# Attention weights normalized on VectorE and transposed in transpose mode, with the products of two heads alternating on halves of the array

## The chip, the cores and the metric

One core of a Trainium2 chip. The metric is device time in microseconds of one execution. TensorE is called PE below, VectorE DVE, ScalarE ACT, GpSimd POOL and SyncE SP, as in the profile. PE's clock is granted at one of two levels, 2.4 GHz (the profile writes 1.00) and 1.2 GHz (0.50).

## The reference

A two-layer decoder trunk over 1040 positions (16 meta tokens and 1024 inputs) of width 1024: a state-space mixer with a gated output, a mixture of experts, sliding-window attention, a second mixture of experts, and a final norm. The change touches the attention:

```python
scale = HEAD_DIM ** -0.5                        # 16 heads of 64, 4 heads of keys and values
s_band = einsum('bnqkgd,bnskd->bnkgqs', qb, k_band) * scale   # own block of 128 and the one before it
s_meta = einsum('bnqkgd,bmkd->bnkgqm', qb, k_meta) * scale    # 16 meta tokens, always visible
s_band = where(band_ok, s_band, NEG)            # 0 <= query position - key position < 128
probs = softmax(concatenate([sink, s_meta, s_band], axis=-1), axis=-1)
o = einsum(p_meta, v_meta) + einsum(p_band, v_band)
return o @ w_o + b_o
```

The sink is one learned logit for each head; it takes part in the sum of the softmax and has no value.

## The kernel before, in words

The program runs its phases one after another with a barrier between them: `phase_ssm`, `phase_glu`, `phase_moe` for layer 0, `phase_project` (keys, values, queries), `phase_attend`, and `phase_moe` for layer 1 with the final norm. Each phase writes out one program for each engine; the order in it is the order in which the engine works, and semaphores join the engines.

`phase_attend` takes 64 steps (`NS`). A step `s` is one query tile of 128 positions (`i = s // 8`) and one pair of heads (`c = s % 8`). Queries and keys stand transposed: the first head of the pair in partitions 0 to 63, the second in 64 to 127. In tile 0 a step has two blocks of keys (the 16 meta tokens and its own block of 128), from tile 1 on three (with the block before). A step goes through:

- PE, `scores(s)`: for each head, a product for every block of keys, with a contraction over 64 rows. The two heads use the two halves of the array's rows.
- DVE, `scores(s)`: adds the mask while reading the scores of both heads (L1888), then takes the negated maximum (L1892), the sink included, which POOL has copied beside the scores (L1831).
- ACT, `exps(s)`: exponentials and their sums, one instruction for each head (L1846).
- DVE, `divisors(s)`: the reciprocals of the sums (L1896), and a diagonal matrix for each head, the identity times the reciprocal (L1900).
- PE, `transpose_weights(s)`: ordinary float32 products of the weights with this diagonal matrix, which transpose and normalize at once (L1963, L1965, L1966).
- ACT, `copy_weights(s)`: copies the transposed weights out of PSUM (L1855, L1856).
- PE, `outputs(s)`: values times transposed weights, three products for each head in one accumulation (L1977, L1979, L1980). Each head has 64 output partitions, that is a half of the array's columns.
- ACT and DVE: `o_hi_part` (L1863) and `o_lo_part` (L1907) split the outputs into two parts for the projection.

`project(i, half)` on PE multiplies a finished tile with half of the output weights, 24 products of 512 columns (L1992 to L1994). DVE adds the result to the residual stream (`add_projection`, L1914). In the first eight steps ACT and DVE also split the output weights that SP loads (L1873, L1928).

The orders are written out by hand. PE: `scores(s + 1)`, `outputs(s - 1)`, `transpose_weights(s)`, and behind the steps `c = 3` and `c = 6` a projection of the tile before. DVE: `o_lo_part(s - 2)`, `divisors(s)`, `scores(s + 1)`, and an addition of a projection at `c = 4` and `c = 7`. ACT: `o_hi_part(s - 2)`, `exps(s)`, `copy_weights(s - 1)`. Scores, weights and their transposed copies are double-buffered; the PSUM tile of the transposes (`ps_t`) and that of the outputs (`ps_o`) are single. POOL adds the output bias to the residual stream once for each tile (L1835).

Of the kernel before, what the change touches and what calls it, by code (L numbers as in the profile page):

```python
# [12 lines left out]
ALU = mybir.AluOpType  # L13
# [1739 lines left out]
def phase_attend(nc, t):  # L1753
# [10 lines left out]
    with ExitStack() as ctx:  # L1764
# [3 lines left out]
        def ps(name, shape):  # L1768
# [5 lines left out]
        mask = sb("mask", [P, SC_W])  # L1774
        sinks = sb("sinks", [P, N_HEADS])
# [8 lines left out]
        diag = sb("diag", [P, 2, H2, P])  # L1784
# [11 lines left out]
        sc_mm, sm_done, nm_done, exp_done, rinv_done, diag_done, pt_mm, pt_done, pv_mm, o_hi_done, o_lo_done, y_mm, h_done = (  # L1796
            sem(x) for x in ("sc_mm", "sm_done", "nm_done", "exp_done", "rinv_done", "diag_done", "pt_mm",
                             "pt_done", "pv_mm", "o_hi_done", "o_lo_done", "y_mm", "h_done"))

        def width(s):  # L1800

            return SC_W if s >= DC else N_META + P
# [13 lines left out]
        def _(pool):  # L1816
# [4 lines left out]
            pool.wait_ge(mask_step, 1)  # L1821
            G_.affine_select(out=mask[:, N_META:N_META + P], in_=mask[:, N_META:N_META + P], compare_op=ALU.is_ge,
                             fill=NEG, base=0, pattern=[[-1, P]], channel_multiplier=1).then_inc(mask_step, 1)
            G_.affine_select(out=mask[:, N_META + P:], in_=mask[:, N_META + P:], compare_op=ALU.is_gt,
# [54 lines left out]
        def _(dve):  # L1879
            V = nc.vector  # L1880

            def scores(s):

                dve.wait_ge(sc_mm, s + 1)
                if s >= 2:
                    dve.wait_ge(exp_done, 2 * (s - 1))
                w = width(s)
                V.tensor_tensor(sm[:, s % 2, :, 1:1 + w], ps_s[:, 2 * (s % 2):2 * (s % 2) + 2, 0:w],  # L1888
                                mask[:, 0:w].unsqueeze(1).to_broadcast([P, H2, w]), ALU.add).then_inc(sm_done, 1)
# [27 lines left out]
            dve.wait_ge(mask_step, 3)  # L1917
            scores(0)
            for s in range(NS):
# [3 lines left out]
                divisors(s)  # L1923
# [14 lines left out]
        def _(pe):  # L1938
            T = nc.tensor

            def scores(s):
# [3 lines left out]
                for r in range(2):  # L1945
                    rows = slice(r * DH, (r + 1) * DH)
                    out = ps_s[:, 2 * (s % 2) + r, :]
                    q = q_t[rows, c, i * P:(i + 1) * P]
                    k = k_t[rows, c // 2, :]
                    T.matmul(out[:, 0:N_META], q, k[:, XT * P:TOK], start=True, stop=True)  # L1950
                    last = T.matmul(out[:, N_META:N_META + P], q, k[:, i * P:(i + 1) * P], start=True, stop=True)
                    if i:
                        last = T.matmul(out[:, N_META + P:SC_W], q, k[:, (i - 1) * P:i * P], start=True, stop=True)  # L1953
                last.then_inc(sc_mm, 1)

            def transpose_weights(s):
                i = s // DC
                pe.wait_ge(diag_done, s + 1)
                if s:
                    pe.wait_ge(pt_done, s)  # L1960
                for r in range(2):
                    p, d = pr[:, s % 2, r, :], diag[:, s % 2, r, :]
                    T.matmul(ps_t[:, r, 0:P], p[:, 1 + N_META:1 + N_META + P], d, start=True, stop=True)  # L1963
                    if i:
                        T.matmul(ps_t[:, r, P:2 * P], p[:, 1 + N_META + P:1 + SC_W], d, start=True, stop=True)  # L1965
                    last = T.matmul(ps_t[0:N_META, r, 2 * P:3 * P], p[:, 1:1 + N_META], d, start=True, stop=True)  # L1966
                last.then_inc(pt_mm, 1)

            def outputs(s):
# [5 lines left out]
                for r in range(2):  # L1975
# [68 lines left out]
```

## Time and profile before

| | |
|---|---|
| median of 3 runs | 2682.65 us (2681.4 to 2683.64) |
| span of the profiled execution | 2682.4 us |
| its own time | given by its span alone; 0.2 us under the median |
| PE busy over the span | 2226.1 us (83%) |
| DVE busy | 1691.0 us (63%) |
| ACT busy | 1242.7 us (46%) |
| POOL busy | 569.7 us (21%) |
| attention phase | from 1488 to 1927 us |

Busy time is what the instructions of an engine cover. Products on PE are pipelined and their recorded lengths overlap, so the time from one start to the next says what one costs. A float32 product is recorded as two passes, each with its own load of the stationary tile (PEld); a product of the rounded float32 form and a transpose in transpose mode are recorded as one.

### The profile page before, as it was taken

What the parts mean: (1) busy time and instruction counts of PE and PEld (TensorE: products, weight loads), DVE (VectorE), ACT (ScalarE), POOL (GpSimd) and SP (SyncE); (2) the same over time, 40 slices, a digit from 0 to 9 for tenths busy, and PEclk for the clock granted to TensorE, in tenths of its full rate; (3) what the DMA queues carried; (4) which work ended last, traced back from release to release, by engine and by line L of the source; (5) the groups of instructions that cost most, each with busy time, mean ns of one, the idle gap of its engine ahead of it and who ended that gap; (6) DMA issues with size and microseconds to landing.
All of it is one profiled execution on the core that took longest, in us unless ns stands there. A gap on an engine that the chain in (4) does not pass through costs nothing. (4 is left out here: it accounts for less than half of the span.)

```text
span 2682.4 us, 32669 instructions
## 1 busy us (share of the span) xinstructions
PE 2226.1 (83%) x11052; PEld 1744.2 (65%) x11052; DVE 1691.0 (63%) x1593; ACT 1242.7 (46%) x1431; POOL 569.7 (21%) x735
## 2 busy tenths in 40 slices
PE   2380489983999999997399999999857999999992
PEld 2130467772788888886288567777655888888881
DVE  6987042126788888885622434444255888888885
ACT  3020341031677777775200323333224777777772
POOL 2105000012233333331210100000021212333333
PEclk9965799966999999998599579999958999999996
DMA  5819550041899999995410200000144999999985
GB/s 157 84 32 84 118 179 32 1 168 56 305 365 376 369 367 372 376 373 222 149 48 24 71 1 1 1 1 1 54 161 142 354 361 372 381 379 377 385 322 234
DMA packets 156509, 527.02 MB, mean 196 GB/s; under 512 B 37072, under 2 KB 87440, under 8 KB 105088
## 3 DMA queue, kind: packets, MB, share of 16 engines
q1 hardware_dynamic: 138000, 492.13, 53.4%
q0 software_dynamic: 18432, 33.86, 3.4%
q8 instruction: 49, 0.80, 0.1%
q14 instruction: 28, 0.23, 0.0%
HBM read 497.42 MB, written 55.71 MB: 206 GB/s over the span
## 5 line engine op out<-in xcount | busy, mean ns | idle before, releaser
L1347 DVE TENSOR_TENSOR moe_lo<-moe_raw,moe_hi 128x2048 fp32r<-128x2048 f32 x378 | 861.6, 2293 | 127.0 <-ACT moe_hi L1152 118.8
L1152 ACT CAST moe_hi<-moe_raw 128x2048 fp32r<-128x2048 f32 x374 | 714.3, 1914 | 154.8 <-PE moe_ps_g L1476 76.1
L1474 PE MATMUL moe_ps_y<-moe_hi,moe_h_hi 128*128 128x512 f32 x512 | 210.0, 410 | 11.0 <-DVE moe_h_lo L1363 11.0
L1474 PE MATMUL moe_ps_g<-moe_hi,moe_x_hi 128*128 128x512 f32 x512 | 212.3, 415 | 7.4 <-DVE moe_x_lo L1352 4.7
L1475 PE MATMUL moe_ps_g<-moe_hi,moe_x_lo 128*128 128x512 f32 x512 | 206.3, 403 | 0.0
L1476 PE MATMUL moe_ps_g<-moe_lo,moe_x_hi 128*128 128x512 f32 x512 | 206.1, 402 | 0.0
L1475 PE MATMUL moe_ps_y<-moe_hi,moe_h_lo 128*128 128x512 f32 x512 | 204.5, 400 | 0.0
L1476 PE MATMUL moe_ps_y<-moe_lo,moe_h_hi 128*128 128x512 f32 x512 | 204.3, 399 | 0.0
L1476 PE MATMUL moe_ps_u<-moe_lo,moe_x_hi 128*128 128x512 f32 x512 | 203.0, 396 | 0.0
L1475 PE MATMUL moe_ps_u<-moe_hi,moe_x_lo 128*128 128x512 f32 x512 | 202.8, 396 | 0.0
L1474 PE MATMUL moe_ps_u<-moe_hi,moe_x_hi 128*128 128x512 f32 x512 | 202.8, 396 | 0.0
L1159 ACT CAST moe_x_hi<-moe_ps_xt 128x1024 fp32r<-128x1024 f32 x64 | 65.0, 1016 | 212.7 <-PE moe_ps_xt L1461 212.7
L785 PE MATMUL glu_acc<-glu_w_hi,glu_z_hi 128*128 128x512 f32 (+1 forms) x288 | 115.6, 401 | 36.2 <-DVE glu_w_lo L750 30.9
L1888 DVE TENSOR_TENSOR att_sm<-att_ps_s,att_mask 128x544 f32<-128x544 f32 (+1 forms) x64 | 44.2, 691 | 146.1 <-PE att_ps_s L1953 133.6
L1096 POOL TENSOR_TENSOR moe_unit<-moe_mhalf 128x1 f32<-128x1 f32 x64 | 20.4, 318 | 508.5 <-DMA y_dram<-moe_y,moe_si 508.5
L1863 ACT CAST att_o_hi<-att_ps_o 128x128 fp32r<-128x128 f32 x64 | 17.0, 265 | 226.3 <-PE att_ps_o L1980 226.3
L1076 POOL COPY moe_gi<-moe_idx_in 128x1 int32 x64 | 80.2, 1254 | 186.3 <-issue 109.3
L1352 DVE TENSOR_TENSOR moe_x_lo<-moe_ps_xt,moe_x_hi 128x1024 fp32r<-128x1024 f32 x64 | 78.4, 1224 | 64.7 <-ACT moe_x_hi L1159 64.7
L1474 PEld LDWEIGHTS moe_ps_g<-moe_hi,moe_x_hi 128*128 128x128 f32 x512 | 99.5, 194 | 30.0 <-DVE moe_x_lo L1352 5.5
L1474 PEld LDWEIGHTS moe_ps_y<-moe_hi,moe_h_hi 128*128 128x128 f32 x512 | 97.8, 191 | 32.6 <-DVE moe_lo L1347 11.4
L1079 POOL TENSOR_TENSOR moe_unit<-moe_mhalf 128x1 f32<-128x1 f32 x128 | 113.6, 888 | 10.8 <-POOL moe_gi L1076 0.2
L787 PE MATMUL glu_acc<-glu_w_lo,glu_z_hi 128*128 128x512 f32 (+1 forms) x288 | 114.4, 397 | 0.0
(347 smaller groups left out, 4660.8 us busy)
## 6 DMA issues: line engine op xcount, KB each, us to landing
moe_raw<-moe_w_gate SPq DMA_DIRECT2D x128, 1024.0 KB, 6.7
moe_raw<-moe_w_up SPq DMA_DIRECT2D x128, 1024.0 KB, 9.2
moe_raw<-moe_w_down SPq DMA_DIRECT2D x128, 1024.0 KB, 8.2
moe_raw<-y_dram SPq DMA_DIRECT2D x16, 1024.0 KB, 11.6
glu_w_raw<-ssm_w_glu SPq DMA_DIRECT2D x8, 1024.0 KB, 5.9
xn_dram<-moe_work SPq DMA_DIRECT2D x16, 512.0 KB, 6.1
u_dram<-ssm_reg SPq DMA_DIRECT2D x8, 520.0 KB, 5.0
ssm_reg<-u_dram SPq DMA_DIRECT2D x8, 520.0 KB, 21.4
```

The lines of the kernel that those rows point to most:

```text
L785: nc.tensor.matmul(out, zh, wh, start=(c == 0), stop=False)
L787: return nc.tensor.matmul(out, zh, wl, start=False, stop=(c == DC - 1))
L1076: G_.tensor_copy(dst[:, :], idx[:, bass.ds(c, 1)]).then_inc(ix_step, 1)
L1079: G_.tensor_tensor(unit[:, 0:1], mhalf[:, :], mhalf[:, :], ALU.mult)
L1152: A.copy(hi[:, slot(number, k), :], raw[:, k, :]).then_inc(hi_done, 1)
L1159: A.copy(x_hi[:, :, :].rearrange("p c m -> p (c m)"), ps_xt[:, :]).then_inc(xt_hi, 1)
L1347: V.tensor_tensor(lo[:, slot, :], raw[:, k, :], hi[:, slot, :].bitcast(F32), ALU.subtract).then_inc(lo_done, 1)
L1352: V.tensor_tensor(x_lo[:, :, :].rearrange("p c m -> p (c m)"), ps_xt[:, :], x_hi[:, :, :].bitcast(F32).rearrange("p c m -> p (c m)"), ALU. ...
L1474: T.matmul(out, x_h, w_h, start=first, stop=False)
L1475: T.matmul(out, x_l, w_h, start=False, stop=False)
L1476: return T.matmul(out, x_h, w_l, start=False, stop=final)
L1888: V.tensor_tensor(sm[:, s % 2, :, 1:1 + w], ps_s[:, 2 * (s % 2):2 * (s % 2) + 2, 0:w], mask[:, 0:w].unsqueeze(1).to_broadcast([P, H2, w]), ...
```

## The change

DVE no longer builds diagonal matrices. `normalize(s)` multiplies the weights of each head in place with the reciprocal of their sum (two instructions over 144 columns in tile 0, 272 from tile 1 on), and PE transposes them in transpose mode against the identity. The order of the columns in the scores changes, so that the block before comes ahead of the own block: both are one product of 256 columns. For tile 0, which has no block before, there is a second mask, `mask0`. In `scores` and `outputs` the two heads' products alternate: the same block for the first head, then for the second. The orders between the steps stay.

```diff
-        diag = sb("diag", [P, 2, H2, P])
+        mask0 = sb("mask0", [P, N_META + P])
...
+            G_.memset(mask0[:], 0.0).then_inc(mask_step, 1)
+            pool.wait_ge(mask_step, 2)
+            for own in (mask0[:, N_META:], mask[:, N_META + P:]):
+                G_.affine_select(out=own, in_=own, compare_op=ALU.is_ge, fill=NEG, base=0, pattern=[[-1, P]],
+                                 channel_multiplier=1).then_inc(mask_step, 1)
+            G_.affine_select(out=mask[:, N_META:N_META + P], in_=mask[:, N_META:N_META + P], compare_op=ALU.is_gt,
                              fill=NEG, base=0, pattern=[[1, P]], channel_multiplier=-1).then_inc(mask_step, 1)
...
-            def divisors(s):
+            def normalize(s):
                 dve.wait_ge(exp_done, 2 * (s + 1))
                 V.reciprocal(rinv[:, s % 2, :], rs[:, s % 2, :]).then_inc(rinv_done, 1)
                 dve.wait_ge(rinv_done, s + 1)
-                if s >= 2:
-                    dve.wait_ge(pt_mm, s - 1)
-                V.tensor_tensor(diag[:, s % 2], ident[:, :].unsqueeze(1).to_broadcast([P, H2, P]),
-                                rinv[:, s % 2, :].unsqueeze(2).to_broadcast([P, H2, P]),
-                                ALU.mult).then_inc(diag_done, 1)
+                for r in range(H2):
+                    p = pr[:, s % 2, r, 1:1 + width(s)]
+                    V.tensor_scalar(p, p, rinv[:, s % 2, r:r + 1], None, ALU.mult).then_inc(norm_done, 1)
...
             def scores(s):
...
-                for r in range(2):
-                    T.matmul(out[:, 0:N_META], q, k[:, XT * P:TOK], start=True, stop=True)
-                    last = T.matmul(out[:, N_META:N_META + P], q, k[:, i * P:(i + 1) * P], start=True, stop=True)
-                    if i:
-                        last = T.matmul(out[:, N_META + P:SC_W], q, k[:, (i - 1) * P:i * P], start=True, stop=True)
+                lo, w = (max(i - 1, 0) * P, min(i + 1, 2) * P)
+                for out, rows in zip(outs, halves):
+                    T.matmul(out[:, N_META:N_META + w], q_t[rows, c, i * P:(i + 1) * P], k_t[rows, c // 2, lo:lo + w],
+                             start=True, stop=True)
+                for out, rows in zip(outs, halves):
+                    last = T.matmul(out[:, 0:N_META], q_t[rows, c, i * P:(i + 1) * P], k_t[rows, c // 2, XT * P:TOK],
+                                    start=True, stop=True)
...
             def transpose_weights(s):
-                    T.matmul(ps_t[:, r, 0:P], p[:, 1 + N_META:1 + N_META + P], d, start=True, stop=True)
+                    T.transpose(ps_t[:, r, 0:P], p[:, own:own + P], ident[:])
                     if i:
-                        T.matmul(ps_t[:, r, P:2 * P], p[:, 1 + N_META + P:1 + SC_W], d, start=True, stop=True)
-                    last = T.matmul(ps_t[0:N_META, r, 2 * P:3 * P], p[:, 1:1 + N_META], d, start=True, stop=True)
+                        T.transpose(ps_t[:, r, P:2 * P], p[:, 1 + N_META:1 + N_META + P], ident[:])
+                    last = T.transpose(ps_t[0:N_META, r, 2 * P:3 * P], p[:, 1:1 + N_META], ident[:])
...
             def outputs(s):
-                for r in range(2):
-                    out, w = ps_o[r * DH:(r + 1) * DH, 0:P], pt[:, s % 2, r, :]
-                    T.matmul(out, v_sb[:, i, vc], w[:, 0:P], start=True, stop=False)
-                    if i:
-                        T.matmul(out, v_sb[:, i - 1, vc], w[:, P:2 * P], start=False, stop=False)
-                    last = T.matmul(out, v_sb[0:N_META, XT, vc], w[0:N_META, 2 * P:], start=False, stop=True)
+                for r in range(H2):
+                    T.matmul(outs[r], v_sb[:, i, vc], w[r][:, 0:P], start=True, stop=False)
+                if i:
+                    for r in range(H2):
+                        T.matmul(outs[r], v_sb[:, i - 1, vc], w[r][:, P:2 * P], start=False, stop=False)
+                for r in range(H2):
+                    last = T.matmul(outs[r], v_sb[0:N_META, XT, vc], w[r][0:N_META, 2 * P:], start=False, stop=True)
```

## Rows read from the trace of the kernel before

**Rows 1.** Stages of attention: window, length, busy time (count) by engine, clock, DMA.
```profile
1499.70:1530.50 30.80, 30.80 (x122) 16.73 (x121) 14.64 (x30) 13.19 (x41) 0.93 (x5) 0.50 0.28 86
1545.60:1563.10 17.50, 17.50 (x74) 11.83 (x72) 4.69 (x11) 4.24 (x14) 0.38 (x3) 0.50 0.00 1
1602.20:1653.10 50.90, 50.90 (x337) 36.42 (x336) 22.00 (x43) 16.95 (x56) 3.83 (x9) 1.00 0.00 1
```
**Rows 2.** Waits from 1480 to 1915: total us, times, longest.
```profile
DVE att_sm L1888 <- PE att_ps_s L1953: 133.6, 56, 8.4
...
PE att_ps_t L1963 <- DVE att_diag L1900: 3.2, 1, 3.2
```
**Rows 3.** Timeline of PE over one step: start, us, then operation.
```profile
1737.34 0.39 PE L1950 MATMUL att_ps_s<-k_t,q_t 64*128 64x16 f32 x2
...
1738.45 0.43 PE L1977 MATMUL att_ps_o<-att_pt,v_sb 128*64 128x128 f32 x2
...
1740.33 0.49 PE L1963 MATMUL att_ps_t<-att_diag,att_pr 128*128 128x128 f32 x2
...
1742.25 0.28 PE L1950 MATMUL att_ps_s<-k_t,q_t 64*128 64x16 f32 x1
```
**Rows 4.** Timeline: transposes in the MoE stage, and column halves in the state stage.
```profile
2020.54 0.27 PE L1453 MATMUL moe_ps_ht<-moe_ident,moe_over 128*1 128x128 f32 x1 [1.32 <-DVE moe_over L1330]
...
2020.65 0.27 PE L1454 MATMUL moe_ps_ht<-moe_ident,moe_over 128*1 128x128 f32 x1
...
133.16 0.67 PE L623 MATMUL ssm_psr<-ssm_reg,ssm_vt 128*64 128x130 f32 x8
133.76 0.33 PE L613 MATMUL ssm_pst<-ssm_ident,ssm_reg 128*128 128x128 f32 x1
```
**Rows 5.** Timeline of DVE and ACT over the same step.
```profile
1738.56 0.72 DVE L1888 TENSOR_TENSOR att_sm<-att_ps_s,att_mask 128x544 f32<-128x544 f32 x1 [1.10 <-PE att_ps_s L1953]
1739.32 0.72 DVE L1892 TENSOR_REDUCE att_nm<-att_sm 128x2 f32<-128x546 f32 x1
...
1740.43 0.27 ACT L1863 CAST att_o_hi<-att_ps_o 128x128 fp32r<-128x128 f32 x1 [2.15 <-PE att_ps_o L1980]
1740.59 0.53 ACT L1846 ACTIVATE att_pr<-att_sm,att_nm 128x273 f32<-128x273 f32 x1
...
1741.75 0.17 DVE L1896 RECIPROCAL att_rinv<-att_rs 128x2 f32<-128x2 f32 x1 [0.73 <-ACT att_pr L1846]
1741.95 0.43 DVE L1900 TENSOR_TENSOR att_diag<-att_ident,att_rinv 128x256 f32<-128x256 f32 x1
...
1742.36 0.59 ACT L1855 COPY att_pt<-att_ps_t 128x512 f32<-128x512 f32 x1 [0.64 <-PE att_ps_t L1966]
1742.84 0.36 ACT L1856 COPY att_pt<-att_ps_t 16x256 f32<-16x256 f32 x1
```
**Rows 6.** Groups by line: scalings on DVE, busy us, mean ns.
```profile
L467 DVE TENSOR_SCALAR ssm_pw_n<-ssm_pw_i 128x288 f32<-128x288 f32 x1 | 0.3, 309 | 0.0
```
**Rows 7.** Timeline of PE over a step at the lower clock.
```profile
1556.29 0.61 PE L1950 MATMUL att_ps_s<-k_t,q_t 64*128 64x16 f32 x2
...
1558.32 0.69 PE L1977 MATMUL att_ps_o<-att_pt,v_sb 128*64 128x128 f32 x2
...
1561.64 0.80 PE L1963 MATMUL att_ps_t<-att_diag,att_pr 128*128 128x128 f32 x2
```
**Rows 8.** Clock and busy time in other stages, columns as in rows 1.
```profile
120.00:154.00 34.00, 28.16 (x284) 17.39 (x280) 27.58 (x52) 11.92 (x30) 0.97 (x1) 1.00 0.17 36
1935.80:1939.20 3.40, 3.40 (x18) 3.40 (x17) 0.84 (x1) 1.63 (x2) 0.00 (x0) 0.50 0.91 255
1939.20:1942.60 3.40, 2.46 (x23) 2.35 (x22) 1.41 (x3) 2.38 (x5) 1.58 (x5) 1.00 0.94 320
1942.60:1963.00 20.40, 20.40 (x100) 20.40 (x99) 6.79 (x9) 8.24 (x12) 7.55 (x27) 0.50 0.96 391
...
2055.20:2058.60 3.40, 3.40 (x9) 2.64 (x8) 2.30 (x2) 0.53 (x1) 0.00 (x0) 0.50 1.03 434
```

More of the change, by code:

```diff
@@ L1795, in phase_attend @@
                              "w_lo_done"))
-        sc_mm, sm_done, nm_done, exp_done, rinv_done, diag_done, pt_mm, pt_done, pv_mm, o_hi_done, o_lo_done, y_mm, h_done = (
-            sem(x) for x in ("sc_mm", "sm_done", "nm_done", "exp_done", "rinv_done", "diag_done", "pt_mm",
+        sc_mm, sm_done, nm_done, exp_done, rinv_done, norm_done, pt_mm, pt_done, pv_mm, o_hi_done, o_lo_done, y_mm, h_done = (
+            sem(x) for x in ("sc_mm", "sm_done", "nm_done", "exp_done", "rinv_done", "norm_done", "pt_mm",
                              "pt_done", "pv_mm", "o_hi_done", "o_lo_done", "y_mm", "h_done"))
@@ L1887, in scores @@
                 w = width(s)
+                visible = mask if s >= DC else mask0
                 V.tensor_tensor(sm[:, s % 2, :, 1:1 + w], ps_s[:, 2 * (s % 2):2 * (s % 2) + 2, 0:w],
-                                mask[:, 0:w].unsqueeze(1).to_broadcast([P, H2, w]), ALU.add).then_inc(sm_done, 1)
+                                visible[:, :].unsqueeze(1).to_broadcast([P, H2, w]), ALU.add).then_inc(sm_done, 1)
                 dve.wait_ge(sm_done, s + 1)
@@ L1916, in _ @@
             dve.wait_ge(ident_step, 2)
-            dve.wait_ge(mask_step, 3)
+            dve.wait_ge(mask_step, 5)
             scores(0)
@@ L1922, in _ @@
                     o_lo_part(s - 2)
-                divisors(s)
+                normalize(s)
                 if s + 1 < NS:
@@ L1944, in scores @@
                     pe.wait_ge(sm_done, s - 1)
-                for r in range(2):
[L1946 to L1949, printed above, removed]
-                    T.matmul(out[:, 0:N_META], q, k[:, XT * P:TOK], start=True, stop=True)
-                    last = T.matmul(out[:, N_META:N_META + P], q, k[:, i * P:(i + 1) * P], start=True, stop=True)
-                    if i:
-                        last = T.matmul(out[:, N_META + P:SC_W], q, k[:, (i - 1) * P:i * P], start=True, stop=True)
+                outs = [ps_s[:, 2 * (s % 2) + r, :] for r in range(H2)]
+                halves = [slice(r * DH, (r + 1) * DH) for r in range(H2)]
+                lo, w = (max(i - 1, 0) * P, min(i + 1, 2) * P)
[5 more added lines that the diff above has]
+                                    start=True, stop=True)
                 last.then_inc(sc_mm, 1)
@@ L1974, in outputs @@
                 vc = slice((c // 2) * DH, (c // 2 + 1) * DH)
-                for r in range(2):
-                    out, w = ps_o[r * DH:(r + 1) * DH, 0:P], pt[:, s % 2, r, :]
-                    T.matmul(out, v_sb[:, i, vc], w[:, 0:P], start=True, stop=False)
-                    if i:
-                        T.matmul(out, v_sb[:, i - 1, vc], w[:, P:2 * P], start=False, stop=False)
-                    last = T.matmul(out, v_sb[0:N_META, XT, vc], w[0:N_META, 2 * P:], start=False, stop=True)
+                outs = [ps_o[r * DH:(r + 1) * DH, 0:P] for r in range(H2)]
+                w = [pt[:, s % 2, r, :] for r in range(H2)]
+                for r in range(H2):
[3 more added lines that the diff above has]
+                        T.matmul(outs[r], v_sb[:, i - 1, vc], w[r][:, P:2 * P], start=False, stop=False)
+                for r in range(H2):
+                    last = T.matmul(outs[r], v_sb[0:N_META, XT, vc], w[r][0:N_META, 2 * P:], start=False, stop=True)
                 last.then_inc(pv_mm, 1)
```

9 lines of the change are left out of this document (3 added, 6 removed).

## The prediction

> **What bounds the kernel now.** I began with the busy rows of the stages of the attention phase [rows 1]. The reader is to see that PE is busy in every microsecond of each of them, while DVE and ACT are busy less than half. The row of a whole query tile lasts 50.9 us with the granted clock at 1.00, that is 2.4 GHz. The first tile (30.8 us for five steps, 6.16 each) and the second tile's first steps (17.5 us for two, 8.75 each) have it at 0.50, 1.2 GHz. Next the waits: the add of the scores on DVE waits for PE, 134 us in all, and PE waits for DVE once, 3.2 us [rows 2]. So PE's own order sets the time of the phase, and nothing outside the phase is touched: a microsecond won there is won at the end.
>
> The timeline of PE over one step, a pair of heads, [rows 3] gives 4.91 us and its parts: scores 1.11 (1737.34 to 1738.45), outputs 1.88 (to 1740.33), transposes 1.92 (to 1742.25). Eight such steps make 39.3 of a tile's 50.9 us, so each of its two projections costs 5.8. Every product appears as two passes (x2), and a 128-column pass takes 0.11 us.
>
> **The change on PE.** *Transposes.* Six products of two passes become six of one: the transposes of the MoE stage start 0.11 us apart with one record each, although their stationary tile is a single column [rows 4], so 0.11 is the price of streaming 128 columns once. 6 x 0.11 = 0.66 off: 1.92 becomes 1.26. Whether the 16-column one still forces a pause between shapes is not shown; without pauses it would be about 0.9, and if the transpose saved nothing 1.92. I take 1.26, the row's form with one pass gone.
> *Outputs.* Today head 0's three products and head 1's three stand one behind the other, 0.94 each. Six passes make only 0.66 of that; the other 0.28 are an uncovered load and two pauses, about 0.09 each, where the shape changes from 128 rows to 16 and back. In the state stage eight passes of 130 columns for the two column halves go through between 133.16 and 133.76 [rows 4]: 0.60 us, pause included, where eight times 0.11 is 0.88. So halves of equal shape overlap; in attention the 16-row product between the heads keeps them apart. Alternating puts equal shapes side by side: 0.94 + 0.03 = 0.97. The other end, no overlap, saves only two of the four changes of shape with their pauses: 1.6.
> *Scores.* The two row halves overlap already, head 1 starting about a quarter microsecond late. Four products instead of six: a head is one load 0.11, two passes of 256 columns (estimate: 2 x 0.21), two short ones with a load, 0.13, and the pause of 0.09, so 0.75, plus 0.06 lag: 0.81. The bound above is today's 1.11.
> PE's sum: 1.26 + 0.97 + 0.81 = 3.04 us, for 4.91.
>
> **The change on DVE, and the new bound.** PE would drop under the loop that runs from exponentials to exponentials, hidden until now. From [rows 5]: exponentials to reciprocal 1741.75 - 1740.59 = 1.16; reciprocal to the next operation 0.20; then the diagonal product (0.43) is replaced by two scalings of 272 columns. A scaling of 288 columns took 0.309 [rows 6]; I take 0.30 for each, less 0.08 that neighbours without a wait between them overlap (an estimate; on ACT L1856 is recorded 0.11 before the end of L1855): 0.44 for the two. The slow end, each scaling at the diagonal's 0.43, adds 0.28. The add of the next scores could then start 1.80 after the exponentials. Add to reduce 0.76, reduce 0.72 and hand-over 0.04: 3.32.
> ACT's loop: two exponentials of 0.51, then the copies 0.48 + 0.36, hand-over 0.12 (estimate), which is 1.98; outputs to the rounding 1.08 (today 1740.43 less the second head's start, half of 1.88 before 1740.33; and 0.03), rounding to exponentials 0.16: 3.22. PE's order adds a tie: it starts outputs at 1.98, ends them at 2.95 and the transposes at 4.21, 0.83 into the next step, so the scores behind them reach DVE at 0.83 + 0.81 + 0.21 = 1.85 instead of 1.80: 3.37. With loops of 3.04, 3.22 and 3.37 so closely interlocked I take a step of 3.4 us; the bounds are 3.3 and, with slow scalings, 3.65, and without overlap of the halves 3.8.
>
> Scaling 0.44 instead of 0.35 for the diagonal was free before under PE's cover; now it is on the path, some 0.1 us in each step. The wait that goes (the diagonal's on the transposes two steps back) was always met. The normalized weights are written in place, so nothing new is queued behind another buffer. GpSimd's addition of the output bias collides with the seventh step's scaling as it did with the diagonal, and lies under the projection, 5.8 us. The second mask is two more GpSimd operations of 0.3 us before the first step: 0.5 us lost once. Operand order of the masks costs nothing.
>
> A step across a projection: when its exponentials start PE has 0.83 of transposes left, then 5.7 of projection, the next scores arrive 1.02 later, and add and reduce follow, 1.52: 9.07. A tile becomes 6 x 3.4 + 2 x 9.07 = 38.5 us for 50.9: 12.4 less, for six tiles 74 us.
>
> **The stretch at 1.2 GHz.** There a step of the second tile splits into scores 2.03, outputs 3.32, transposes 3.4 [rows 7]. The same cuts: transposes less 6 x 0.21 = 2.1, outputs 1.7, scores 1.5: 5.3, over DVE's loop, so PE sets it. The first tile's 6.16 becomes 4.0 by the same working with two thirds of the products. Gains: five steps of 2.1 in the first tile, 10 (the first two are start-up); two mixed ones after it, 4.7; three of the second tile at 3.1 (the first is partly narrow), 9.3; the step with the first projection 1.5 only, because the projection may have to bring the clock up: in the MoE stage it stood at 0.50 through a row of dense products (the row at 2055.2) [rows 8]. The rest of the tile has the full clock, four steps of 1.5: 6. Together 31 us.
>
> **Sum.** 74 + 31 - 0.5 = 104.5, and about 1 for the tail, of a span of 2682.4; the median of the runs shown, 2682.65, is 0.2 us above it. I forecast 2580 us rather than 2577, the tight interlocking costing a few hundredths of a microsecond in each step.
>
> **Rivals.**
> 1. *Halves don't overlap, or slow scalings.* For: the two streams read all 128 rows at once with full weights here. Against: [rows 4]. With a step of 3.8 a tile is 6 x 3.8 + 2 x 9.47 = 41.7, six tiles give 55 and the slow stretch, where the outputs keep 2.9 of their 3.3, some 19: 2608. Slow scalings alone, a step of 3.65, give 2592; both together about 2625.
> 2. *The clock falls between projections.* PE would for the first time have gaps, about a tenth of each step. For: in the row at 1939.2 the clock was 1.00 with PE busy 2.46 of 3.4 us, and in the next it is 0.50 again. Against: from 120 to 154 us it stayed at 1.00 with PE busy 28.2 of 34 us, in a loop of transposes and half-width products like the new step; and it rose right behind 3.4 us in which nearly all of PE's 18 records were transposes (the row at 1935.8) [rows 8]. If it falls, a step costs 5.3, 1.9 more, and a projection that has to bring the clock back costs 3 more (up to 6 us at half speed, an estimate from the row at 2055.2). With n such steps a tile is 38.5 + 1.9 n + 6. The 31 us won in the slow stretch allow a tile of 56, so it decides from six steps of the eight: 2683 there, 2706 with all eight. This is the case on the other side.
> The Trainium skill, "TensorE: Matmul & The Clock Gate", Part 4, says that transposes do not count as activity for the clock, which speaks against this change. By that rule rival 2 would happen. The trace does not agree: the clock rose behind the row at 1935.8, where PE was busy 3.40 of 3.40 us with transposes.
> 3. *An earlier rise.* Denser passes bring 1.00 already in the second tile's first steps: 10 us less, 2570.
> 4. *The change doesn't do what it says*: transposes go through in two passes. PE then needs 3.7 and holds the copy up: a step of 3.95, 2614.
>
> **Chances.** Forecast, 2566 to 2597: 0.62. Rival 3, 2555 to 2566: 0.07. Rival 1, 2592 to 2625: 0.16. Rival 4: 0.04. Rival 2 in part, up to 2677: 0.06; from six steps on 0.05, of which 0.01 within the measurement's reach of 2683. The range leaves out rival 2 above 2628 and what lies below rival 3: 2555 to 2628, 0.85. What a measurement of this kernel can tell from no change is 0.2%, 5.4 us. Faster 0.94, same 0.02, slower 0.04, the last two from rival 2.
>
> **What the profile after would show.** A tile of 38.5 us with clock 1.00; transposes as single records 0.11 apart; heads' outputs starting within 0.05 of each other; PE for the first time waiting, about 0.35 us a step, mostly before the outputs or the transposes; DVE busy 2.4 of 3.4 us; scalings of 0.30. Wrong would be: the two heads' outputs 0.5 or more apart in their ends, scalings of 0.44, PEclk under 1.00 between 1600 and 1850 us, or a wait I don't see, such as DVE held by GpSimd's copies in every step.

## The result and the profile after

The changed kernel takes 2554.08 us (median of 4 runs, 2552.01 to 2557.14) against 2683.14 (4 runs, 2681.40 to 2686.24) beside it: a ratio of 0.952, 95% interval 0.9506 to 0.9533. It is 129 us faster, where 103 were forecast, and it lies 1 us under the forecast's range of 2555 to 2628. Its profiled execution has a span of 2552.1 us and a time of 2553.88, so the profile speaks for the runs.

First the same stages as in [rows 1], now of the changed kernel: most of tile 0, the two rows of the profile on either side of the clock's rise, and one whole tile from its first reduce to that of the next. The columns are the length, then the busy time of each engine with its number of instructions, the granted clock, and the DMA share.

```profile
core 0: us, PE busy (x) PEld busy (x) DVE busy (x) ACT busy (x) POOL busy (x), PEclk, DMA share, GB/s
1500.00:1522.10 22.10, 21.78 (x131) 13.60 (x132) 20.38 (x46) 16.85 (x50) 3.42 (x7) 0.50 0.45 143
1525.80:1529.20 3.40, 3.40 (x22) 2.69 (x22) 1.92 (x6) 2.15 (x7) 0.19 (x1) 0.50 0.00 0
1529.20:1532.60 3.40, 2.69 (x32) 1.97 (x28) 2.44 (x7) 2.11 (x7) 0.19 (x1) 1.00 0.00 0
1559.65:1596.61 36.96, 31.77 (x260) 23.80 (x256) 22.36 (x51) 16.92 (x56) 3.85 (x9) 1.00 0.00 1
```

A tile lasts 36.96 us instead of 50.90, and PE, busy without a gap before, now idles for 5.2 us of it. The clock rises at 1529.2 us, in the third step of tile 1; before, it stood at 0.50 until 1574.0, when the first projection ran.

The waits of the attention phase, in answer to [rows 2]: total, times, longest.

```profile
ACT att_o_hi L1865 <- PE att_ps_o L1985: 133.3, 63, 5.8
DVE att_sm L1891 <- PE att_ps_s L1953: 49.7, 17, 4.7
DVE att_rinv L1899 <- ACT att_pr L1848: 47.6, 56, 1.0
PE att_ps_o L1980 <- ACT att_pt L1858: 37.5, 43, 1.6
```

DVE waited 133.6 us for scores; now it does so 17 times, nearly all behind the projections, and in the steps between it waits for the exponentials. PE waits in 43 steps for the copied weights. In a step of tiles 1 to 7 that crosses no projection, each of PE, DVE and ACT now waits for another: no engine is the bound, a chain through two of them is.

PE over one step right behind a projection, where its parts stand close together as in [rows 3] (start, length):

```profile
1668.87 0.70 PE L1950 MATMUL att_ps_s<-k_t,q_t 64*128 64x256 f32 x4
1669.41 0.29 PE L1953 MATMUL att_ps_s<-k_t,q_t 64*128 64x16 f32 x4
1669.63 0.44 PE L1980 MATMUL att_ps_o<-att_pt,v_sb 128*64 128x128 f32 x4
1669.90 0.39 PE L1983 MATMUL att_ps_o<-att_pt,v_sb 128*64 128x128 f32 x4
1670.22 0.43 PE L1985 MATMUL att_ps_o<-att_pt,v_sb 16*64 16x128 f32 x4
1670.59 0.33 PE L1965 MATMUL att_ps_t<-att_ident,att_pr 128*128 128x128 f32 x1
1670.75 0.27 PE L1967 MATMUL att_ps_t<-att_ident,att_pr 128*128 128x128 f32 x1
1670.86 0.27 PE L1968 MATMUL att_ps_t<-att_ident,att_pr 128*16 128x128 f32 x1
1670.97 0.27 PE L1965 MATMUL att_ps_t<-att_ident,att_pr 128*128 128x128 f32 x1
...
1671.39 0.49 PE L1950 MATMUL att_ps_s<-k_t,q_t 64*128 64x256 f32 x2
```

Scores 0.76, outputs 0.96, transposes 0.80: 2.52 us for 4.91. The transposes are single records, and the 16-column one (L1968) is followed after 0.11 like every other.

The loop through DVE and ACT, from exponentials to exponentials, in answer to [rows 5]; first DVE, then ACT:

```profile
1672.42 0.17 DVE L1899 RECIPROCAL att_rinv<-att_rs 128x2 f32<-128x2 f32 x1 [0.39 <-ACT att_pr L1848]
1672.62 0.63 DVE L1903 TENSOR_SCALAR att_pr<-att_pr,att_rinv 128x272 f32<-128x272 f32 x2
1673.17 0.72 DVE L1891 TENSOR_TENSOR att_sm<-att_ps_s,att_mask 128x544 f32<-128x544 f32 x1
1673.92 0.72 DVE L1895 TENSOR_REDUCE att_nm<-att_sm 128x2 f32<-128x546 f32 x1
```

```profile
1671.27 0.53 ACT L1848 ACTIVATE att_pr<-att_sm,att_nm 128x273 f32<-128x273 f32 x1 [0.30 <-DVE att_nm L1895]
1672.29 0.56 ACT L1857 COPY att_pt<-att_ps_t 128x512 f32<-128x512 f32 x1
1674.68 0.52 ACT L1848 ACTIVATE att_pr<-att_sm,att_nm 128x273 f32<-128x273 f32 x1 [0.18 <-DVE att_nm L1895]
```

It takes 1.15 us from the exponentials to the reciprocal, 0.20 to the scalings, 0.55 to the add, 0.75 to the reduce and 0.76 to the next exponentials: 3.41 in all, which is the plain step. A step across a projection takes 8.24 (a crossing, below), and six of the one and two of the other make the tile.

**Where the 130.3 us between the two spans come from**, by the starts of the reduces (a tile is eight intervals between them):

| stretch | before | after | change | forecast |
|---|---|---|---|---|
| up to the first reduce | 1491.0 | 1494.0 | +3.0 | +0.5 |
| tile 0 | 44.6 | 28.1 | -16.4 | -10 |
| tile 1 | 66.6 | 37.6 | -29.1 | -21 |
| tiles 2 to 7, to the end of the phase | 325.1 | 240.3 | -84.9 | -75 |
| second mixture of experts | 755.1 | 752.1 | -3.0 | 0 |

The last row is the same code in both, and so is nearly all of the first: in the twelve kernels below the attention phase starts between 1486.6 and 1494.3 us, and the last phase takes 751.6 to 754.8 (755.1 before is just above). I take both rows for scatter. The 0.5 us that the forecast charged for the second mask did not appear: from the first scores to the first reduce it is 2.84 us before and 2.85 after, because the reduce waits for the copied sinks in both. The forecast's two steps of mixed width, 4.7 us, stand in its row of tile 1; by the reduces one of them (7.27 us before, 5.33 after) lies in tile 0.

### The profile page after: what moved, and what is told of

The parts are those of the page before. It is cut to its first block and busy times, and to the rows that moved or that the text cites. A ratio compares the mean times of both kernels' runs of the same rounds, so it can differ in the third digit from the quotient of the medians.

```text
span 2552.1 us, 31490 instructions
## 1 busy us (share of the span) xinstructions
PE 2056.5 (81%) x10460; PEld 1636.8 (64%) x10460; DVE 1693.2 (66%) x1657; ACT 1242.0 (49%) x1431; POOL 564.4 (22%) x737
## 5 line engine op out<-in xcount | busy, mean ns | idle before, releaser
L1096 POOL TENSOR_TENSOR moe_unit<-moe_mhalf 128x1 f32<-128x1 f32 x64 | 16.4, 256 | 514.1 <-DMA y_dram<-moe_y,moe_si 514.1
L1476 PEld LDWEIGHTS moe_ps_g<-moe_lo,moe_x_hi 128*128 128x128 f32 x512 | 98.9, 193 | 24.2
L786 PE MATMUL glu_acc<-glu_w_hi,glu_z_lo 128*128 128x512 f32 (+1 forms) x288 | 114.1, 396 | 0.0
L1079 POOL TENSOR_TENSOR moe_unit<-moe_mhalf 128x1 f32<-128x1 f32 x128 | 111.5, 871 | 10.7
```

The lines of the kernel that those rows point to most:

```text
L786: nc.tensor.matmul(out, zl, wh, start=False, stop=False)
L1079: G_.tensor_tensor(unit[:, 0:1], mhalf[:, :], mhalf[:, :], ALU.mult)
L1476: return T.matmul(out, x_h, w_l, start=False, stop=final)
```

## The experiments

All are edits of the changed kernel; every step that TensorE, VectorE or ScalarE takes for the output stays. The table has the medians, the ratio to before with its interval, the plain step and the step across a projection of tiles 2 to 7, and when the clock rose in the attention phase.

| kernel | us | ratio | step | across | clock 1.00 at |
|---|---|---|---|---|---|
| changed kernel | 2554.1 | 0.9520 (0.9506 to 0.9533) | 3.41 | 8.24 | 1529.2 |
| a_diag_alternate | 2600.5 | 0.9690 (0.9674 to 0.9706) | 3.88 | 9.67 | 1540.4 |
| b_transposes_alone | 2616.6 | 0.9757 (0.9740 to 0.9773) | 4.05 | 9.51 | 1555.6 |
| c_outputs_serial | 2606.1 | 0.9716 (0.9699 to 0.9732) | 4.05 | 9.16 | 1551.8 |
| e_scores_serial | 2560.9 | 0.9543 (0.9527 to 0.9559) | 3.41 | 8.58 | 1544.2 |
| d_one_scaling | 2554.1 | 0.9523 (0.9510 to 0.9536) | 3.50 | 8.15 | 1529.4 |
| f_scores_first | 2543.2 | 0.9484 (0.9469 to 0.9498) | 3.13 | 8.12 | 1527.4 |
| h_three_orders | 2526.4 | 0.9407 (0.9393 to 0.9422) | 2.52 | 8.32 | 1542.8 |
| g_transposes_x4 | 2555.3 | 0.9525 (0.9511 to 0.9540) | 3.41 | 8.24 | 1503.0, lost 1530.3 to 1533.8 |
| i_fill_whole | 2523.9 | 0.9404 (0.9389 to 0.9418) | 2.52 | 8.32 | 1501.6 |
| j_fill_half | 2557.7 | 0.9531 (0.9517 to 0.9546) | 2.52 | 8.32 | 1578.7 |
| k_after_again | 2556.2 | 0.9528 (0.9515 to 0.9541) | 3.41 | 8.24 | 1527.4 |
| l_fill_less | 2525.1 | 0.9403 (0.9384 to 0.9423) | 2.52 | 8.32 | 1495.0, lost 1522.3 to 1546.2 |

### One part undone at a time

**a_diag_alternate**: the diagonal back in place of the scalings.

```diff
-                for r in range(H2):
-                    p = pr[:, s % 2, r, 1:1 + width(s)]
-                    V.tensor_scalar(p, p, rinv[:, s % 2, r:r + 1], None, ALU.mult).then_inc(norm_done, 1)
+                V.tensor_tensor(diag[:, s % 2], ident[:, :].unsqueeze(1).to_broadcast([P, H2, P]),
+                                rinv[:, s % 2, :].unsqueeze(2).to_broadcast([P, H2, P]), ALU.mult).then_inc(norm_done, 1)
...
-                    T.transpose(ps_t[:, r, 0:P], p[:, own:own + P], ident[:])
+                    T.matmul(ps_t[:, r, 0:P], p[:, own:own + P], d, start=True, stop=True)
```

> The changed kernel with its alternating outputs and merged scores, but with the diagonal product on VectorE and ordinary transposing products on TensorE, as before. If the parts measured on TensorE simply add (scores 0.76, outputs 0.96, transposes back at 1.92), TensorE needs 3.64 us a step and is never idle: a tile of 8 x 3.64 + 2 x 5.8 = 40.7 us instead of 36.96, some 25 us over tiles 1 to 7, so about 2580 us if the clock still rises during tile 0, and about 2605 if the early rise came from the transpose mode and is lost with it. Rival: the loop through VectorE alone sets the step and the transposes were free already; then the step stays at 3.3 to 3.4 and the time at or under 2555.

Measured: 2600.5 us, 46 more than the changed kernel. The step behind a projection is 3.64, the sum of the parts to the hundredth, but the others take 3.88. The trace shows why:

```profile
1579.83 0.49 PE L1968 MATMUL att_ps_t<-att_diag,att_pr 128*128 128x128 f32 x2
...
1581.87 0.59 ACT L1858 COPY att_pt<-att_ps_t 128x512 f32<-128x512 f32 x1 [0.47 <-PE att_ps_t L1971]
...
1582.76 0.44 PE L1983 MATMUL att_ps_o<-att_pt,v_sb 128*64 128x128 f32 x4 [0.17 <-ACT att_pt L1859]
...
1583.71 0.49 PE L1968 MATMUL att_ps_t<-att_diag,att_pr 128*128 128x128 f32 x2
```

Transposes 2.04 with the hand-over, copies 0.89, outputs 0.95: a loop of 3.88 through PE and ACT, longer than PE's sum, because the scores (0.76) that PE does meanwhile are shorter than the hand-over and the copies. The expectation that the parts simply add was short by it; the rival, in which the transposes were free, falls. The clock rose 11 us later than in the changed kernel, but at the same place in the work: while PE worked on the third set of wide scores of tile 1 or on the outputs right behind it, ahead of the projection. So the early rise does not need the transpose mode.

**b_transposes_alone**: scores and outputs back in the order of before (`+ for r in range(H2):` around all three products of a head, in both). **c_outputs_serial**: the outputs alone:

```diff
                 for r in range(H2):
                     T.matmul(outs[r], v_sb[:, i, vc], w[r][:, 0:P], start=True, stop=False)
-                if i:
-                    for r in range(H2):
+                    if i:
                         T.matmul(outs[r], v_sb[:, i - 1, vc], w[r][:, P:2 * P], start=False, stop=False)
-                for r in range(H2):
                     last = T.matmul(outs[r], v_sb[0:N_META, XT, vc], w[r][0:N_META, 2 * P:], start=False, stop=True)
```

> Only the scalings and the transposes of the change; scores and outputs in the order of before. TensorE's parts would be 0.80 + 1.88 + 1.11 = 3.79 a step; the loop through ScalarE (exponentials 1.02, copies 0.84, outputs 1.88, rounding to exponentials 0.2, hand-overs 0.1) would be about 4.05. If the loop holds, a step of 4.05 and a tile of about 42.5 us: 2590 us with an early rise of the clock, about 2630 if the rise needs the alternating halves (then it comes as late as before, near 1574 us). If only TensorE's sum matters, a step of 3.8 and some 10 us less.

> The changed kernel with only the outputs back in serial order, one head behind the other. TensorE's sum is 0.76 + 1.88 + 0.80 = 3.44, no more than today's step of 3.41: if TensorE's sum or VectorE's loop is what counts, the time stays near 2560 us. If the loop through ScalarE counts, in which the outputs lie, the step is 4.05 and the time some 35 to 40 us above 2554, near 2590. For the clock: if alternating output halves are what raised it during tile 0, it rises late here, and the time is up to 35 us more on top.

Both have a step of 4.05, though PE's sums are 3.79 and 3.44. The clock rose in the first projection in both, and the times lie between what was expected for an early and for a late rise. Of c, ACT with the outputs that it waits for:

```profile
1605.55 0.27 ACT L1865 CAST att_o_hi<-att_ps_o 128x128 fp32r<-128x128 f32 x1 [2.04 <-PE att_ps_o L1983]
1605.71 0.53 ACT L1848 ACTIVATE att_pr<-att_sm,att_nm 128x273 f32<-128x273 f32 x1
...
1606.73 0.57 ACT L1857 COPY att_pt<-att_ps_t 128x512 f32<-128x512 f32 x1
...
1607.61 0.43 PE L1980 MATMUL att_ps_o<-att_pt,v_sb 128*64 128x128 f32 x2 [0.53 <-ACT att_pt L1858]
...
1608.55 0.43 PE L1980 MATMUL att_ps_o<-att_pt,v_sb 128*64 128x128 f32 x2
...
1609.59 0.27 ACT L1865 CAST att_o_hi<-att_ps_o 128x128 fp32r<-128x128 f32 x1 [2.04 <-PE att_ps_o L1983]
```

Rounding to exponentials takes 0.16, exponentials 1.02, copies 0.88, the first head 0.94, and the second head 1.04 to the rounding: 4.04. So the alternation is worth 0.64 us a step (4.05 to 3.41) by ACT's loop and next to nothing by PE's sum (3.44). It also shows that the halves overlap: 0.96 for both heads where each takes 0.94 alone.

**e_scores_serial**: the scores alone, three products a head, one head behind the other.

```diff
                 for out, rows in zip(outs, halves):
-                    T.matmul(out[:, N_META:N_META + w], q_t[rows, c, i * P:(i + 1) * P], k_t[rows, c // 2, lo:lo + w],
-                             start=True, stop=True)
-                for out, rows in zip(outs, halves):
...
+                    for b in range(0, w, P):
+                        last = T.matmul(out[:, N_META + b:N_META + b + P], q_t[rows, c, i * P:(i + 1) * P],
+                                        k_t[rows, c // 2, lo + b:lo + b + P], start=True, stop=True)
```

> The changed kernel with only the scores as before: three products a head, one head behind the other. TensorE waits about 0.9 us in each step before the outputs, so 0.35 us more for the scores is hidden inside a step: step 3.41. Behind a projection the scores are waited for, so each of the 14 crossings costs 0.35 more: 5 us, 2559 us. Rival: the scores are on the path in every step, 3.76 us: about 2575 us.

The step stays at 3.41 and the crossings are 0.34 longer, as expected; the rival's 3.76 did not come. Of the 6.8 us, the crossings are about 5 (14 of 0.34). The rest lies at 1.2 GHz, where the longer scores show in each step (3.45 in tile 0 for 3.26, 5.17 in tile 1), and in the clock, which rose 15 us later, in the first projection.

### The loops, and a kernel without them

**d_one_scaling** makes one product over both heads (544 columns) of the two scalings:

```diff
-                for r in range(H2):
-                    p = pr[:, s % 2, r, 1:1 + width(s)]
-                    V.tensor_scalar(p, p, rinv[:, s % 2, r:r + 1], None, ALU.mult).then_inc(norm_done, 1)
+                p = pr[:, s % 2, :, 1:1 + w]
+                V.tensor_tensor(p, p, rinv[:, s % 2, :].unsqueeze(2).to_broadcast([P, H2, w]), ALU.mult).then_inc(norm_done, 1)
```

> The changed kernel with the two scalings as one operation over both heads (a product of two tensors, 544 columns). The mask's add has that form and takes 0.72 us, where the two scalings together hold VectorE 0.55. If VectorE's loop (exponentials to reciprocal 1.15, 0.20, scaling, add 0.75, reduce 0.76) sets the step, it grows by about 0.17 to 3.58 and the time by some 8 us to 2562. If TensorE's order or ScalarE's loop sets it, which have margin, the step stays 3.41 and the time 2554.

The step grew by 0.09, which is what the scaling grew by in DVE's order:

```profile
1677.38 0.72 DVE L1903 TENSOR_TENSOR att_pr<-att_pr,att_rinv 128x544 f32<-128x544 f32 x1
1678.02 0.72 DVE L1891 TENSOR_TENSOR att_sm<-att_ps_s,att_mask 128x544 f32<-128x544 f32 x1
```

0.64 to the next operation, not 0.72, against 0.55 for the pair: the direction was right, the size half. The crossings became 0.09 shorter, so a tile grows by only 0.37 us (37.32 for 36.95), and the time, 2554.1 where 2562 was expected, tells nothing; the step in the trace does.

**f_scores_first** opens that loop, and **h_three_orders** ACT's as well. f:

```diff
             scores(0)
+            scores(1)
...
-                if s + 1 < NS:
-                    scores(s + 1)
+                if s + 2 < NS:
+                    scores(s + 2)                      # PE
...
-                normalize(s)
                 if s + 1 < NS:
                     scores(s + 1)                      # DVE
+                normalize(s)
```

h adds to f: on PE `transpose_weights(s)` ahead of `outputs(s - 1)`; on ACT `exps(s)`, `copy_weights(s - 1)`, `o_hi_part(s - 2)`; on DVE `o_lo_part(s - 2)` last.

> The changed kernel with the scores two steps ahead on TensorE, and VectorE adding and reducing the next pair's scores before it scales this pair's weights. This opens VectorE's loop. What is left is ScalarE's loop: exponentials 1.02, copies 0.84, hand-over 0.07, outputs 0.96, rounding 0.3, about 3.15 to 3.2 a step. If VectorE's loop is what sets 3.41 now, the step falls to about 3.2 and the time to about 2540. If ScalarE's loop or TensorE's order is already at 3.4, nothing is won: 2554.

> As the kernel with scores two ahead, and ScalarE's loop opened too: ScalarE copies the transposed weights before it rounds the outputs, TensorE transposes before it makes the outputs, and VectorE takes the low parts last. No loop goes through two engines' whole work any more; the engines' own sums are TensorE 2.52, VectorE 2.55, ScalarE 2.2. If the loops were the bound, the step falls to about 2.65 and a tile to 32.6 us: about 2524 us. If something else holds the step (access to the same memory by several engines, GpSimd), it stays above 3: 2540 or more. Another danger: a tile of TensorE gaps no longer than these can still lose the clock.

f has 3.13 us a step and takes 2543.2 us. In its trace ACT starts a rounding every 3.13 us, at 1612.62 and 1615.75, each 0.16 ahead of the exponentials; with 1.03 of exponentials, 0.87 of copies, 0.95 of outputs and 0.12 to the next rounding that is ACT's loop. h has 2.52 a step, less than the 2.65 expected. The window of one of its tiles and the outputs of two steps in a row:

```profile
1552.92:1584.68 31.76, 31.76 (x258) 23.83 (x260) 21.50 (x51) 16.96 (x56) 3.86 (x11) 1.00 0.01 1
```

```profile
1600.46 0.44 PE L1980 MATMUL att_ps_o<-att_pt,v_sb 128*64 128x128 f32 x4
...
1601.41 0.70 PE L1950 MATMUL att_ps_s<-k_t,q_t 64*128 64x256 f32 x4
...
1602.17 0.33 PE L1965 MATMUL att_ps_t<-att_ident,att_pr 128*128 128x128 f32 x1
...
1602.97 0.44 PE L1980 MATMUL att_ps_o<-att_pt,v_sb 128*64 128x128 f32 x4
```

PE is the bound again, with the 2.52 us of its parts and never idle. 2526.4 us is 28 less than the changed kernel: this is what the cuts on PE were worth and the loops held back. At 1.2 GHz PE's own sums set the step: in tile 0 it took 3.26 in the changed kernel, in f and in h alike, and in tile 1 it took 4.54 in h.

### The clock

**g_transposes_x4** makes each transpose of tile 0 four times over.

```diff
-                for r in range(H2):
+                for r in [r for r in range(H2) for _ in range(1 if i else 4)]:
                     p = pr[:, s % 2, r, :]
                     T.transpose(ps_t[:, r, 0:P], p[:, own:own + P], ident[:])
```

> The changed kernel with every transpose of the first tile made four times, to see what transposes do for the clock. It adds 12 transposes a step in the first tile, about 2.5 us at 1.2 GHz. If transposes count for the clock like products, TensorE is now busy without a gap in the first tile, the clock rises there, and steps fall to about 4; tile 0 some 35 us. If they don't count, the clock stays at 0.50 through the first tile, whose steps are 5.5 to 5.8, 18 to 20 us more in all, about 2573 us, and it rises in the second tile at the earliest, as without the copies.

```profile
1499.60:1503.00 3.40, 3.40 (x19) 2.65 (x16) 1.98 (x5) 1.07 (x5) 0.19 (x1) 0.50 0.51 154
1503.00:1506.40 3.40, 3.24 (x34) 2.46 (x32) 2.39 (x5) 2.60 (x8) 0.22 (x1) 1.00 0.17 67
```

```profile
1499.76 0.48 PE L1965 MATMUL att_ps_t<-att_ident,att_pr 128*128 128x128 f32 x1
...
1502.80 0.37 PE L1965 MATMUL att_ps_t<-att_ident,att_pr 128*128 128x128 f32 x1
```

Between 1499.76 and 1503.0 PE did nothing but transposes, at 0.50, and the clock rose right behind them, 26 us earlier than in the changed kernel. It stayed up through the tile and fell for one row only, at 1530.3 in tile 1, behind a row in which PE was busy 2.09 of 3.40 us. The 96 added transposes cost tile 0 only 3 us more than the changed kernel's (31.4 for 28.1), because the rest of it ran at 1.00. The Trainium skill, "TensorE: Matmul & The Clock Gate", Part 4, says that transposes don't count as activity for the clock; the trace does not agree.

**i_fill_whole** and **j_fill_half** add products to h's first tile whose result nobody uses, on all 128 rows of the array or on 64. **l_fill_less** has fewer of i's.

```diff
+            def fill(n):
+                for _ in range(n):
+                    T.matmul(ps_y[:, :], q_t[0:P, 0, 0:P], k_t[0:P, 0, 0:512], start=True, stop=True)   # i; j: 0:DH
...
                     scores(s + 2)
+                if s < DC:
+                    fill(6 if s < 2 else 2)            # l: fill((6, 3)[s] if s < 2 else 1)
```

> The kernel with the three orders changed (2526 us), with products added in the first tile whose result nobody uses: 128 rows by 128 columns of the array, 512 columns streamed, six ahead of the transposes in each of the first two steps, where TensorE waits for ScalarE and VectorE, and two a step in the other six. If whole-array work brings the clock up or keeps it up, the granted clock is 1.00 in the first tile and the second tile's steps take 2.5 us from the start: tile 0 some 25 us, tile 1 some 31 instead of 36.5, about 2519 us. If the added work only costs time, tile 0 grows by some 10 us at 1.2 GHz and the time to about 2535.

> The same, but the added products use 64 rows of the array instead of 128; they stream the same 512 columns and should take the same time at the same clock. If what counts for the clock is that TensorE is busy, this kernel gives the same clock and time as the one with whole-array products, about 2519 us. If half-used rows count for less, which would explain why before held 1.2 GHz for 80 us with TensorE never idle, the clock stays at 0.50 through the first tile and rises in the second or with the projection: about 2535 us.

> The kernel with added whole-array products, with fewer of them: six in the first step, three in the second, one in each of the other six of the first tile. With two a step TensorE itself set the first tile's step, 3.64 us at the full clock, 0.95 of it the added products. With one it needs 2.7 and VectorE (sum of its rows about 3.0 with the splitting of the output weights) sets some 3.1: tile 0 about 27 us instead of 32.6, tile 1 stays 27, in all about 2519 us. Rival: the clock needs the second product as well and falls in the first tile; then tile 0 is 28 to 30 us and tile 1 up to 36, 2526 us or more, and nothing is left of the gain.

The windows of i (the row ahead of the rise, the rest of tile 0 from 1508, tile 1), then of j:

```profile
1498.20:1501.60 3.40, 3.40 (x5) 1.33 (x4) 1.07 (x5) 1.57 (x4) 2.50 (x2) 0.50 0.68 271
...
1508.00:1529.70 21.70, 21.70 (x133) 11.74 (x133) 14.99 (x36) 13.21 (x40) 2.76 (x6) 1.00 0.37 122
...
1529.76:1556.84 27.08, 26.84 (x224) 19.16 (x224) 20.90 (x50) 17.41 (x57) 3.35 (x10) 1.00 0.01 2
```

```profile
1510.40:1544.50 34.10, 34.10 (x116) 15.07 (x114) 11.65 (x28) 11.18 (x34) 1.76 (x4) 0.50 0.19 62
1544.50:1578.70 34.20, 34.20 (x155) 20.58 (x154) 17.72 (x39) 15.24 (x49) 3.89 (x8) 0.50 0.00 1
1578.70:1582.10 3.40, 3.40 (x16) 2.76 (x15) 0.00 (x0) 0.00 (x0) 0.00 (x0) 1.00 0.00 0
```

The two kernels stream the same columns at the same places. With 128 rows the clock is 1.00 from 1501.6 us on. With 64 rows PE is busy in every microsecond from 1510.4 to 1578.7, in tile 0 (to 1547.7) with the added products and then with the kernel's own, and the clock stands at 0.50 all the while; it rises only with the first projection, whose products use the whole array. j is 34 us slower than i, and 23 slower than was expected for this outcome; in the profiled executions its tile 0 takes 23 us more than i's (55.3) and its tile 1 15 more (42.4). So a busy PE is not enough, and what differs between the two is the rows in use. That fits the kernel before, which ran from 1495.0 to 1573.9 us with PE never idle at 1.2 GHz: its scores use half of the rows and its outputs half of the columns. It is not the whole answer. The same steps hold 3.4 us of transposing products on the whole array, and half of the columns was not tried by itself.

As a gain the filling fails: i's tile 1 takes 27.1 us instead of h's 36.5, but its tile 0 32.6 instead of 25.8, and 2523.9 us is the same as h's 2526.4 within the intervals, where 2519 was expected. l, with fewer added products, kept 1.00 through tile 0 and lost it when PE waited at the change of tiles:

```profile
1498.40:1518.80 20.40, 20.40 (x149) 11.68 (x146) 15.86 (x37) 16.68 (x51) 3.40 (x7) 1.00 0.45 145
1518.80:1522.20 3.40, 1.82 (x16) 0.77 (x14) 3.35 (x7) 2.50 (x7) 1.88 (x2) 1.00 0.00 0
1522.30:1542.80 20.50, 19.77 (x105) 13.84 (x106) 11.77 (x30) 9.85 (x33) 0.93 (x5) 0.50 0.01 2
```

Behind a row with PE busy 1.82 of 3.40 us the clock is 0.50, and the gain is gone: 2525.1 us, about the time of its rival, though the rival had the clock fall in tile 0. Its five runs spread from 2517.8 to 2531.5, more than any other kernel's.

**k_after_again** is the changed kernel once more.

> The changed kernel itself once more, on the same chip as the two above. If the clock's early rise is a property of its work, it rises in the third step of the second tile again (1525 to 1533 us), and the time is 2554 within 3 us; if it was the luck of one execution, some runs are about 6 us longer, with the rise in the first projection.

The rise came at 1527.4, again in the third step of tile 1, and tiles 0 and 1 took 28.14 and 37.56 us (28.13 and 37.55 before). The time, 2556.2 (2553.0 to 2558.4), is within what was expected. So the early rise is not the luck of one execution. That every run has it is not shown: the slowest of the five is 5 us above the fastest and left no trace.

## Why the forecast came out 26 us too high

**Right.** PE set the time and fell below a loop through DVE and ACT: f shows it, which opens the loop with PE's work unchanged and gains 0.28 us a step. The outputs were put at 0.97 and measured 0.96, the scores at 0.81 and measured 0.76. The halves overlap, which c shows, so the first half of rival 1 is out. The transposes are single records 0.11 apart, so rival 4 is out. ACT's loop was put at 3.22: f, which is left with it, measures 3.13, and c, with 0.9 more of outputs in it, 4.05. The scores are hidden inside a step, as e shows. Rival 2, the clock falling between projections, did not happen: it stayed at 1.00 from 1529.2 to 1785.2 us with PE busy 31.77 of 36.96 in a tile.

**Right in part by luck.** The step was forecast at 3.4 and measured 3.41. The loop that sets it is the one through DVE, forecast at 3.32. Its scalings cost 0.55 and not 0.44, which makes it 3.41; the tie through PE's order, which lifted the forecast to 3.37, did not bind, and 0.03 more were a round-up. The two errors nearly cancel.

**Wrong, and by how much.** The table's forecast adds up to 105.5 us, and the spans differ by 130.3. Tiles 2 to 7 and the tail give 10 of the missing 25, tile 1 gives 8, tile 0 gives 6; the first and the last row of the table cancel. The 3 us that the forecast added on top (2580 rather than 2577) for tight interlocking did not come either, the plain step being 0.01 over 3.4.

1. *"Whether the 16-column one still forces a pause between shapes is not shown ... I take 1.26, the row's form with one pass gone."* This is the step that failed: a term of the sum was taken too large. Of the two ends named there, 1.26 and about 0.9, the low one was nearly right. The transposes stand 0.11 apart across the 16-column one, and cost 0.80 with the hand-over to the scores, 0.63 when the projection follows. In a plain step this is hidden. It shows where PE is the bound. Across a projection the exponentials were to find 0.83 us of transposes ahead of them on PE; they found 0.07, as these rows of PE and of ACT at a crossing show, and 0.63 of this 0.76 is what the term was too large by. With scores that arrive 0.88 behind the projection instead of 1.02, and 5.77 for it instead of 5.7, that is the whole difference of 9.07 and 8.24, and twelve crossings make the 10 us. In a, whose transposes cost 1.92, a crossing is 1.43 longer.

```profile
1663.07 0.27 PE L1968 MATMUL att_ps_t<-att_ident,att_pr 128*16 128x128 f32 x1
1663.10 0.48 PE L1997 MATMUL att_ps_y<-att_wo_hi,att_o_hi 128*128 128x512 f32 x1
```

```profile
1663.03 0.52 ACT L1848 ACTIVATE att_pr<-att_sm,att_nm 128x273 f32<-128x273 f32 x1 [0.18 <-DVE att_nm L1895]
```

2. *"The first tile's 6.16 becomes 4.0"* and *5.3 for the second*: it is mostly the same term at 1.2 GHz. PE's sum there is 3.26 and 4.54 (the latter from h). Of the 4.54, the transposes are 1.48 where 2.1 was forecast, the scores 1.39 for 1.5 and the outputs 1.67 for 1.7. In tile 0 the five steps for which 10 us were forecast gave 14.6 (5.96 and four of 6.16 became 2.98 and four of 3.26); the other 1.9 is the mixed step named below the table.
3. *"An earlier rise"*, rival 3, given a chance of 0.07, took place. The clock rose in the third step of tile 1, 45 us earlier by the time and ahead of the projection with which it came before. It was priced at 10 us. What it is worth in the changed kernel is an estimate: had it waited for the projection, two steps of tile 1 would have taken h's 4.54 instead of 3.41, and the crossing 1.9 more (10.49 in e's tile 1, 8.58 in its later ones), some 4 us of tile 1's 8. The rest there is points 1 and 2. By this estimate points 1 and 2 without the rise would have left the kernel near 2558, inside the range.
   What brought the rise is shown in part. Added products on 128 rows brought 1.00 within tile 0 and added products on 64 rows did not (i, j), and added transposes brought it too (g). With the scores or the outputs serial it waited for the projection (e, c, b), so in this kernel both alternations were needed. But h, with the changed kernel's products in another order, waited for the projection as well in its profiled execution, and why is open. One of h's four runs took 2517.8 us, 8 less than the next; that is about what an early rise would be worth there (i's tile 1 is 9.4 shorter), but the run left no trace.
4. *Two scalings at 0.44*: 0.55. The forecast's slow end for them, two at 0.43, would add 0.26 and not the 0.28 that it names; the truth lay between. It cost 0.05 us a step against the tie: the add was to start 1.85 us after the exponentials for PE's sake, and starts 1.90 after them for the scalings' sake alone, the scores having long arrived.

## What to carry to other kernels

When the bounding engine's work is cut below its neighbours', write down each loop that goes through two engines and comes back, with the order in which each engine's program stands; the longest is the new step, however idle every engine looks. Changing only the order of the calls on three engines was worth another 28 us here, while 0.34 us more of scores on PE changed nothing in a plain step (e). A pause seen between two kinds of instruction in one mode of an engine need not exist in another: price the row with and without it, and see which stretches (here the crossings and the steps at 1.2 GHz) have the engine as the bound and will show the difference. Where the clock is at its lower level although PE is busy, it is worth trying what the products' use of the array does, as i and j do.

## What was not expected of the hardware

- PE busy without a gap did not by itself bring 2.4 GHz: with products added on 64 rows it stayed at 1.2 GHz for a whole tile and beyond, 68 us without a gap (j). With the same stream on 128 rows, which began at 1497.4, PE had 2.4 GHz from 1501.6 on (i).
- The clock rose right behind 3.2 us in which PE did nothing but transposes in transpose mode (g), 26 us earlier than without the added ones.
- Transposes of 16 and of 128 columns follow each other without a pause, 0.11 us apart, where the outputs' change from 128 to 16 rows does cost a pause: 0.21 us from the last pass of the one (1661.90) to the first of the other (1662.10), passes of one shape being 0.11 apart.
- An operation on VectorE with a broadcast operand over 544 columns is recorded with 0.72 us but lets the next begin after 0.64; two of 272 columns take 0.55 together (d).
